# Seven block products in place of eight for the gate and up tiles of a fp32 feed-forward

## What is computed

```python
def swiglu(h, w_in, w_out):
    g, u = jnp.split(h @ w_in, 2, axis=-1)
    return (jax.nn.silu(g) * u) @ w_out
...
hs = modulate(rms_norm(xs, norm2_w[i]), mod_s[3], mod_s[4])
xs = xs + mod_s[5] * swiglu(hs, ffn_in_w[i], ffn_out_w[i])
```

## Time and profile before

| | us |
|---|---|
| median of 3 runs | 2666.12 (2665.93 to 2666.26) |
| the profiled execution | 2665.85 |
| its span | 2664.2 |
| TensorE busy, matmuls | 2651.6, 17638 |
| VectorE busy | 1718.7 |
| ACT busy | 862.8 |
| GpSimd busy | 94.0 |

### The profile page before, as it was taken

How to read it: one execution, slowest core, us unless ns; L and a number is a source line. 1 busy time by engine, 2 the same in 40 slices (tenths; PEclk the granted TensorE clock), 3 DMA queues, 4 the chain that set the end, 5 groups by cost and what they waited for, 6 DMA issues and landing times.

```text
span 2664.2 us, 45828 instructions
## 1 busy us (share of the span) xinstructions
PE 2651.6 (100%) x17638; PEld 2581.8 (97%) x17638; DVE 1718.7 (65%) x2908; ACT 862.8 (32%) x1185; POOL 94.0 (4%) x185
## 2 busy tenths in 40 slices
PE   9999999999999999999999999999999999999998
PEld 5999999999999999999968999999999999999998
DVE  5898778686587777746675778676465554334345
ACT  4223332322342122125665431322332233233122
POOL 0000001000000000000000001000000000000000
PEclk9999999999999999999999999999999999999999
DMA  8443345344223444422002235443122212222212
GB/s 308 142 146 138 127 140 174 124 162 132 77 85 129 161 144 134 142 67 86 33 13 88 96 133 174 132 144 119 64 87 71 79 64 79 79 71 71 79 65 70
DMA packets 85604, 294.95 MB, mean 111 GB/s; under 512 B 10112, under 2 KB 13312, under 8 KB 85248
## 3 DMA queue, kind: packets, MB, share of 16 engines
q1 hardware_dynamic: 60016, 200.74, 22.5%
q0 software_dynamic: 25488, 92.81, 10.4%
HBM read 290.63 MB, written 2.88 MB: 110 GB/s over the span
## 4 chain that ended last, share of the span: by engine, by line
PE 96%; DVE 2%; ACT 1%; DMA 1%; issue 0%; DVEq 0%; ACTq 0%; SPq 0%
PE ps L464 45%; PE ps L465 45%; PE ps_x L678 1%; PE ps L654 1%; PE ps L810 1%; PE ps_sum L665 1%; DMA mix<-in_ada_head 1%; DVE w_lo L1236 1%; PE ps L761 0%; ACT w_hi L872 0%; PE ps L535 0%; PE ps_sum L640 0%; DVE g_lo L1250 0%; ACT g_hi L884 0%; DVE tmp L1312 0%
## 5 line engine op out<-in xcount | busy, mean ns | idle before, releaser
L1236 DVE TENSOR_TENSOR w_lo<-raw,w_hi 128x1024 fp32r<-128x1024 f32 (+2 forms) x359 | 429.1, 1195 | 634.0 <-ACT w_hi L872 632.0
L872 ACT ACTIVATE w_hi<-raw 128x1024 fp32r<-128x1024 f32 (+2 forms) x359 | 371.9, 1036 | 973.2 <-PE ps L465 967.1
L464 PE MATMUL ps<-h_hi,w_hi 128*128 128x320 f32 x1888 | 590.2, 313 | 0.7 <-DVE h_lo L1396 0.7
L465 PE MATMUL ps<-h_lo,w_hi 128*128 128x322 f32 x1888 | 586.5, 311 | 0.0
L464 PE MATMUL ps<-h_hi,w_lo 128*128 128x320 f32 x1888 | 586.3, 311 | 0.0
L465 PE MATMUL ps<-h_hi,w_lo 128*128 128x322 f32 x1888 | 585.8, 310 | 0.0
L465 PE MATMUL ps<-h_hi,w_hi 128*128 128x322 f32 x1888 | 584.6, 310 | 0.0
L464 PE MATMUL ps<-h_lo,w_hi 128*128 128x320 f32 x1888 | 583.9, 309 | 0.0
L1264 DVE CUSTOM_DVE_ANT_0 ps_x<-ada_w,cond 128x1024 f32<-128x1024 f32 x354 | 435.9, 1231 | 28.5 <-DVE tmp L1312 13.2
L465 PEld LDWEIGHTS ps<-h_hi,w_hi 128*128 128x128 f32 x1888 | 359.0, 190 | 0.6
L465 PEld LDWEIGHTS ps<-h_hi,w_lo 128*128 128x128 f32 x1888 | 358.2, 190 | 0.0
(11 more groups left out here) (179 smaller groups left out, 2887.9 us busy)
## 6 DMA issues: line engine op xcount, KB each, us to landing
raw<-in_weights SPq DMA_DIRECT2D x323, 512.0 KB, 3.3
ada_w<-in_ada_w POOLq DMA_DIRECT2D x177, 512.0 KB, 3.5
raw<-in_weights SPq DMA_DIRECT2D x32, 384.0 KB, 3.0
mix<-in_ada_head SPq DMA_DIRECT2D x16, 512.0 KB, 10.3
x<-in_x SPq DMA_DIRECT2D x8, 320.0 KB, 9.9
out_y<-mix SPq DMA_DIRECT2D x16, 160.0 KB, 1.9
mix<-in_spread SPq DMA_DIRECT2D x1, 1088.0 KB, 5.5
cond<-in_cond SPq DMA_DIRECT2D x1, 1024.0 KB, 13.6
```

The source lines that it names most:

```text
L464: pe.matmul(ps[:, 2 * slot, 0:TA], w[:, slot, ws], a(k)[:, 0:TA], start=begin, stop=end)
L465: mm = pe.matmul(ps[:, 2 * slot + 1, 0:width - TA], w[:, slot, ws], a(k)[:, TA:width], start=begin, stop=end)
L872: act.activation(w_hi[:, j % 2, 0:tiles * P], raw[:, j, 0:tiles * P] if src is None else src, ACT.Copy).then_inc(w_hi_ready, 1)
L1236: dve.tensor_tensor(w_lo[:, j % 2, 0:tiles * P], raw[:, j, 0:tiles * P] if src is None else src, w_hi[:, j % 2, 0:tiles * P].bitcast(F32), ...
```

## The change

For each pair, gate tile and up tile are taken as the two block rows, k = 0 to 3 and 4 to 7 as the inner blocks, and the two column halves of `h` as the two block columns, each 322 wide (the first takes two columns of the second along). Eight products of half a weight tile (128 x 512) become seven, by Strassen's scheme in the form with few sums. Of each pair, three blocks are parts of the weights as they are (1, 2, 4) and four need sums (S1 to S4: 5, 7, 6, 3). The sums of `h` (T1 to T4) are made once for each layer. All 22 pairs of layers 0, 2 and 3 go this way and the last 14 of the pooling layer's.

The order of the blocks is pairs (p, block). GpSimd makes the weight sums, and its loads of `ada_w` are placed between them:

```diff
+def _order(n):
+    out = [(0, 1), (0, 5), (0, 2), (0, 6), (0, 3), (0, 7)]
+    for p in range(1, n):
+        out += [(p, 1), (p - 1, 4), (p, 5), (p, 6), (p, 2), (p, 7), (p, 3)]
+    return out + [(n - 1, 4)]
...
+            def s13(layer, c, p, q, n, norm):
...
+                    pool.wait_ge(block_lo_ready, SEVEN * first + PLACE[n][p - 1, 5] + 1)
...
+                pool.tensor_tensor(s1_home(p, norm), up_w[:, 0:HW], up_w[:, HW:2 * HW], ALU.add).then_inc(s_made, 1)
+                pool.wait_ge(block_lo_ready, SEVEN * first + PLACE[n][p, 1] + 1)
+                pool.wait_ge(s_made, 4 * (first + p) + 1)
+                pool.tensor_tensor(up_w[:, 0:HW], gate_w[:, 0:HW], up_w[:, 0:HW], ALU.subtract).then_inc(s_made, 1)
+            def s24(layer, c, p, n, norm):
...
+                pool.wait_ge(s_made, 4 * (first + p) + 2)
+                pool.tensor_tensor(gate_w[:, 0:HW], s1_home(p, norm), gate_w[:, 0:HW], ALU.subtract).then_inc(s_made, 1)
+                pool.wait_ge(block_lo_ready, SEVEN * first + PLACE[n][p, 2] + 1)
+                pool.wait_ge(s_made, 4 * (first + p) + 3)
+                pool.tensor_tensor(gate_w[:, HW:2 * HW], gate_w[:, HW:2 * HW], gate_w[:, 0:HW], ALU.subtract).then_inc(s_made, 1)
...
+            def rest_of_chunk(layer, c, q, n, norm, triples):
+                for p in range(1, n):
+                    if p % 2 == 1 and p > 1 and p // 2 < len(triples):
+                        ada_triple(triples[p // 2])
+                    s13(layer, c, p, q, n, norm)
+                    s24(layer, c, p, n, norm)
```

TensorE takes the blocks in the fixed order; slots of `w_hi` and `w_lo` are halved, so four blocks are ahead:

```diff
+                def product(p, m, out, a_hi, a_lo, begin, row_ready=None):
+                    b = place[p, m]
+                    pe.wait_ge(block_lo_ready, SEVEN * first + b + 1)
...
+                    for k in range(HALF):
...
+                        for i, (w, a) in enumerate(((hi, a_hi), (hi, a_lo), (lo, a_hi))):
+                            mm = pe.matmul(out, w[:, ws], a[:, k, :], start=begin and k == 0 and i == 0,
+                                           stop=k == HALF - 1 and i == 2, skip_group_check=True)
+                    mm.then_inc(seven_done, 1)
```

ACT copies each block high (`block_hi`), copies the results of products 1, 5 and 6 into SBUF, and applies SiLU and the hidden split as before. VectorE, for each pair p (a `refill` is the low half of the block four places on, `block_lo`):

```diff
+                def after_p1(p):
+                    refill(p, 1)
+                    modulation(p, 0)
...
+                for p in range(1, n):
+                    after_p1(p)
+                    after_p4(p - 1)
+                    refill(p - 1, 4)
+                    hidden(p - 1)
+                    refill(p, 5)
+                    after_p6(p)
+                    hidden_lo(p - 1)
+                    after_p2(p)
+                    after_p7(p)
...
+                    after_p3(p)
+                after_p4(n - 1)
```

T1 to T4: GpSimd sums rows of `h_hi` and `h_lo` back and combines them (3 sums of 322 columns for each k of T1, 5 for each k of the others), ACT and VectorE split the results inside the last output quad before the first chunk. The last row's five sums are done by VectorE, each waiting for the one before:

```diff
+            def turn_last(layer):
...
+                own(dve.tensor_tensor(t3_full[:, k, :], h_hi[:, m, TA:TH].bitcast(F32), h_lo[:, m, TA:TH].bitcast(F32), ALU.add))
+                own(dve.tensor_tensor(t2_full[:, k, :], t3_full[:, k, :], t2_full[:, k, :], ALU.subtract))
...
+                if c == FIRST_SEVEN[layer]:
+                    turn_last(layer)
+                    t234_lo_of(layer, HALF - 1)
```

More of the change, by code:

```diff
@@ L98, with _slots, _refill, _pairs_before @@
 TH = T + 2
-ROW = T + 4
+ROW = T + 8
+TW = TA + 2
+HALF = KD // 2
+HW = HALF * P
+T_PITCH = TW + 2
+T3_AT = TW + 2
+SEVEN = 7
+T_STEPS = 4 * HALF
+def _order(n):
[3 more added lines that the diff above has]
+    return out + [(n - 1, 4)]
+def _slots(n):
+    jump = (SEVEN * n // 8) * 4
+    return [(b if SEVEN * n % 4 == 0 or b < jump else b + 2) % 4 for b in range(SEVEN * n)]
+def _refill(n):
+    slots = _slots(n)
+    out, last = [[] for _ in range(SEVEN * n)], 0
+    for b in range(4, SEVEN * n):
+        last = max(last, max(c for c in range(b) if slots[c] == slots[b]))
+        out[last].append(b)
+    return out
+ORDER = {n: _order(n) for n in (CHUNK, LAST)}
+PLACE = {n: {pm: b for b, pm in enumerate(ORDER[n])} for n in ORDER}
+SLOT = {n: _slots(n) for n in ORDER}
+REFILL = {n: _refill(n) for n in ORDER}
+FIRST_SEVEN = [1 if kind == "pool" else 0 for kind in KIND]
+LAYER_S = [sum(FT - CHUNK * FIRST_SEVEN[n] for n in range(i)) for i in range(DEPTH + 1)]
+def _pairs_before(layer, c):
+    return LAYER_S[layer] + CHUNK * (c - FIRST_SEVEN[layer])
 H_BASE = [KD * n for n in range(2 * DEPTH)]
@@ L852, in _ @@
                     tiles = CHUNK if c < 2 else LAST
-                    h_quads(q, 2 * layer + 1, tiles // 2, first=(c == 0), late=(c == 0 and kind == "pool"))
+                    if c < FIRST_SEVEN[layer]:
+                        h_quads(q, 2 * layer + 1, tiles // 2, first=True, late=True)
+                    else:
+                        seven_chunk(layer, c, q, tiles, c == 0)
                     q += tiles // 2
@@ L910, in out_quad @@
+            def out_quad(q, m0, n, tiles, squares, folds=True, first=None, turns=None):
                 for j in range(4):
@@ L914, in out_quad @@
                         step(q, j, tiles[j])
+                        if first is not None and j >= 2:
+                            first_blocks(*first, j)
                     if squares:
@@ L1350, in out_quad @@
+            def out_quad(q, m0, n, gate, tiles, squares, folds=True, ada=None, triples=1, first=None, turns=None):
                 for j in range(4):
```

512 lines of the change are left out of this document (449 added, 63 removed).

## The result

The changed kernel takes 2918.75 us (median of 4, 2915.53 to 2921.07) against 2666.02 (4 runs beside it), a ratio of 1.0947 [1.0928, 1.0966]: 252.7 us slower, where +63 was forecast. The profiled execution has a span of 2918.4 us, 254.2 more than before.

A forecast was written before the change was run, and what follows sets the result against it. TensorE bounds the kernel, busy in 2651.6 of 2664.2 us; VectorE becomes the bound in pairs with modulation sums. Terms -139 + 44 + 75 - 25 + 88 + 20 = +63 give 2729 us, range 2595 to 2860.

The forecast's parts named there:

- TensorE, -139: All 80 pairs: 84 matmuls for 96, 12.4 us for 14.16, saving 1.74 us a pair, -139 us.
- Rival D: Products don't come at the old pace, so nothing is saved: +202, 2868 us; chance 0.03.
- VectorE is the bound, +44: 40 pairs with modulation sums: VectorE needs 13.5 us against TensorE's 12.4, 1.1 us more a pair, +44 us.
- Blocking, +88: GpSimd's sums hold up VectorE for half of 4.4 us, 2.2 us in each of 40 pairs, +88 us.
- 3.0 us of slack: Pairs without modulation sums: VectorE needs 9.4 us against TensorE's 12.4, so they pay nothing for blocking.
- Rival A: GpSimd's sums and VectorE's two-input work exclude each other fully: +204, 2870 us; chance 0.14.
- Fifteen waits for loads, +75: VectorE waits for `ada_w` loads queued behind S4, 5.0 us, three times a chunk in five chunks, +75 us.
- The credit of -25 for chunk edges: Four filled blocks and output products at a chunk's beginning absorb some 5 us in each of five chunks, -25 us.
- sign of a VectorE that binds: Expected in the profile after: TensorE's weight load waits for VectorE's `w_lo` in the chunks of layers 0 to 2.
- The start, +20: Feed-forward start in layers 0, 2 and 3: last row's sums 5 us late, 2 for backlog, 7 x 3, about +20 us.

The follow-up runs named there:

- e2: Changed kernel with GpSimd's four weight sums a pair made one-column memsets and block 5 taken straight from the up tile; 2766.33 us.
- e13: Changed kernel with all weight sums on VectorE, GpSimd keeping the loads and the sums of rows; 2841.09 us.
- e7: Changed kernel with GpSimd's 27 sums of rows a layer made 11 memsets of 322 columns and 16 of one; 2866.51 us.
- e11: Seven products only in layer 3's chunks 1 and 2, rows turned one output quad earlier, last row by GpSimd too; 2652.89 us, 0.9951 of the kernel before.
- e9: Seven products only in layer 3's chunks 1 and 2, all other chunks as in the kernel before; 2664.06 us, 0.9993 of that kernel.
- e3: Changed kernel with GpSimd's four weight sums a pair made memsets of the same 512 columns, writing as much but reading nothing; 2777.21 us.
- e6: Changed kernel with loads issued ahead of S4, and weight sums and the chunks' modulation sums made one-column memsets; 2639.82 us.

## Why the prediction was wrong

The direction held, the size did not: +252.7 for +63, and above the range. By its own terms:

- **TensorE, -139: right.** 12.50 us a pair where nothing else binds (e2, layer 3 chunk 1), so 1.70 a pair against the 1.74 taken, -136. Rival D, no pace, is out.
- **VectorE is the bound, +44: work near the forecast, the term too large.** Without blocking 9.26 us a pair in layer 3 (74.11 / 8, forecast 9.4) and 12.84 with modulation sums (102.75 / 8, forecast 13.5). Over TensorE's 12.50 that leaves 0.34 a pair, 14 us in place of 44.
- **Blocking, +88: the size of one was right, its reach was not.** 2.3 us a pair measured by VectorE's busy time, 2.2 taken; a sum alone takes 1.28, not 1.1. But taking it out, with GpSimd's time, gave 152 us. By the table's e2 column, 114 of it is in the (m) chunks, not 88, and 33 in the other chunks, to which the prediction gave nothing because they had "3.0 us of slack": layers 0 to 2 chunk 2 lose 6 to 10 us each. Another 7 is in the output quads. Slack as an average over a pair doesn't cover a block that comes late. Rival A (+204, 2870 us) priced the blocking at 229 and was nearest in total, but for the wrong reason: it took the whole 4.4 us of sums for a loss. The engines do exclude each other, but of 5.1 us of sums a pair (4 x 1.28) VectorE lost 2.3; for the rest it was in other work or waiting.
- **Fifteen waits for loads, +75: right**, 15 times 5.3 us (80.1 in all), in the place and order forecast. Taking them out gave 57, since part of what was saved went into more blocking.
- **The credit of -25 for chunk edges: wrong, and a term was missing.** In a chunk VectorE was to be busy 125.6 us (13.5 + 2.2, eight times) and is busy 123.6. It was to wait 15 less 5, and is idle for 26.1: 16.0 for loads, 8.3 for ACT's copies, the rest small. The wait for copies was in no term. It is not GpSimd's doing: it is 8.6 us in e2 and 8.0 in e13, where GpSimd makes no weight sum. The timeline shows how it comes about. At 570.11 us VectorE is done with a low half and the next block isn't copied yet, because ACT first splits the hidden row and copies product 6 (ACT, then VectorE):

```profile
569.54 0.74 ACT L1312 ACTIVATE g_hi<-tmp 128x640 fp32r<-128x640 f32 x1 [1.49 <-DVE tmp L1909]
...
570.50 1.14 ACT L1239 ACTIVATE w_hi<-raw 128x512 fp32r<-128x512 f32 x2
```

```profile
571.15 0.69 DVE L1791 TENSOR_TENSOR w_lo<-raw,w_hi 128x512 fp32r<-128x512 f32 x1 [1.05 <-ACT w_hi L1239]
```

  GpSimd's sums do hold up ACT (105.1 and 81.2 us in all behind S2 and S4, L602 and L606), but how much of that reaches VectorE or TensorE no run shows.

  Sixteen us more of idle time and two less of work make 14 us a chunk, which in five chunks is about the 66 us that the (m) chunks lacked (forecast +112, measured +178). The prediction's sign of a VectorE that binds, TensorE waiting for `w_lo`, hardly came either (2.6 of 36 us in this chunk): TensorE waited for results to be read out of PSUM by ACT and VectorE, a path the prediction doesn't have.
- **The start, +20: the step that failed most, 100.** The prediction counted the last row only (5 us behind, 2 for the backlog), and took the earlier rows' sums as done in time. GpSimd's 22 sums before the chunk, at 0.9 to 1.9 us each, make the output quad in front longer by 44 us in four layers, and the third group's splits and the last row's chain hold TensorE for 56 more in the chunk. e7 shows the first, and that 11 of the 56 go with GpSimd's sums too; e11 shows the second in the one place where it was tried, layer 3 chunk 1 of e9, and for the other chunks it is argued from the timeline. Which of two ways makes the output quad longer is not settled: there VectorE is busy 53.9 us where it was 45.9, and ACT also waits for GpSimd's rows (34.4 us, 12 times); e7 takes both away.

In sum, +66 in the (m) chunks, +44 in the others (forecast -70, measured -26, of which e2 gives back 33; the last chunks of a layer keep 10 more over 12.50 us a pair in e2, and the pace of 12.50 is 2), and +80 at the start are the 190 us missing. It is time in which work was late or held up, not work that was left out of the count.

## What to carry to other kernels

Before work goes from a busy VectorE to GpSimd, price it on both: here four two-input sums of 0.7 us, moved, held VectorE up for 2.3 to 2.6 us a pair where making them itself costs 2.6, and made a third stop for every block that needs one. Once a bound engine also waits for links of a chain (a load behind a sum, a copy behind a sum), add those waits, nearly at full length (57 of 80 us here); grant no slack that is only an average. A scheme that trades TensorE's work for VectorE's pays where VectorE has room (here two chunks of the last layer, 0.5%), and its set-up belongs a stage earlier than its use.

## What the runs showed of the hardware

- Blocked instructions come in steps. Of 560 low halves of 512 columns 428 take under 0.7 us, 9 between 0.7 and 1.1, and 123 more than that, up to 1.78, most of these 1.3 to 1.4; in e2 555 take under 0.7. GpSimd's sum of L595 takes from 1262 to 2216 ns, median 1817. Both engines wait, and the waiting is listed as busy time:

```profile
L595 POOL TENSOR_TENSOR raw<-raw x80: 1262/1817/2216, 276.3 to 2846.5; 128x512 f32<-128x512 f32 x80
L1791 DVE TENSOR_TENSOR w_lo<-raw,w_hi x480: 676/686/1775, 272.9 to 2857.9; 128x512 fp32r<-128x512 f32 x160
```

- Memsets of 512 columns on GpSimd (0.53 us, e3) slow nothing: VectorE's low half stays at 693 ns.
- VectorE reading PSUM for one of its inputs is not held up: 482 ns for 322 columns in the mean of 80 (L1876), 493 at most. A multiplication of 320 columns with both inputs in SBUF (L1900) takes 491 to 1058 ns.
- The mean granted clock is lower where TensorE has gaps: 0.90 in layer 0 chunk 1 after, 0.93 in e2, 1.00 in e6, where TensorE hardly stops, and 1.00 in layer 3 chunk 1, idle for 2.3 of 103.58 us. TensorE's busy time goes with it (113.51 against 100.20 us for the same products). How much of the chunk's length that adds was not tried: TensorE idles there for 36 us all the same.
